# First mixer by scaled tokens and a later shift, second key chunk's weights in front of the second shift slice

## What is computed

```python
mod_l = (silu_c @ mod_w[i] + mod_b[i]).reshape(bsz, N_MOD, 1, D_MODEL)
mod_c = (silu_cc @ mod_w[i] + mod_b[i]).reshape(N_MOD, 1, D_MODEL)
h_lat = modulate(rms_norm(lat, norm_g[i, 0]), mod_l[:, 0], mod_l[:, 1])
h_ctx = modulate(rms_norm(cx, norm_g[i, 0]), mod_c[0], mod_c[1])
...
z = h.astype(jnp.float32) @ w_in
q, k, v, r, glr = jnp.split(z, [...], axis=-1)
g = jax.nn.log_sigmoid(jnp.einsum('blzr,zrk->blzk', glr, w_gate) + b_gate) / GLA_GATE_NORM
```

## Time and profile before

| | |
|---|---|
| median of 3 runs | 1206.23 us (1205.76 to 1207.28) |
| the profiled execution | 1206.26 us, of it 1204.5 us span |
| PE busy | 1158.5 us, 96% of the span |
| DVE busy | 741.7 us, 62% |
| ACT busy | 556.6 us, 46% |
| POOL busy | 113.6 us, 9% |
| mean granted clock of PE | 0.992 |
| DMA | 209.42 MB, mean 174 GB/s |

### The profile page before, as it was taken

One profiled execution on the slowest core, in us unless ns is written; L12 is line 12 of the kernel. 1 busy time (PEld: TensorE's weight loads), 2 busy tenths in 40 slices (PEclk: granted clock), 3 DMA queues, 4 the chain that ended last, 5 costly groups with the idle time before them and its releaser, 6 DMA issues.

```text
span 1204.5 us, 19086 instructions
## 1 busy us (share of the span) xinstructions
PE 1158.5 (96%) x7472; PEld 1005.1 (83%) x7476; DVE 741.7 (62%) x1048; ACT 556.6 (46%) x760; POOL 113.6 (9%) x109
## 2 busy tenths in 40 slices
PE   5899998899999989999999999999999999999997
PEld 2587775699999988648999999999999988999996
DVE  2887335697554586745465456776667776654653
ACT  3753232634333453644343346666666655433432
POOL 1000051187100070000000000000000000000000
PEclk9999999899999999999999999999999999999999
DMA  9674464977755540708554635555555434745500
GB/s 352 222 268 165 137 241 105 323 226 241 213 181 179 172 99 1 279 2 282 207 185 168 222 105 144 137 141 156 157 157 157 147 130 161 271 170 205 190 19 36
DMA packets 200241, 209.42 MB, mean 174 GB/s; under 512 B 6027, under 2 KB 167190, under 8 KB 199990
## 3 DMA queue, kind: packets, MB, share of 16 engines
q1 hardware_dynamic: 196480, 197.41, 51.3%
q0 software_dynamic: 2928, 9.02, 2.7%
q10 hardware_dynamic: 774, 2.17, 0.5%
HBM read 207.53 MB, written 2.01 MB: 174 GB/s over the span
## 4 chain that ended last, share of the span: by engine, by line
PE 90%; DVE 4%; ACT 2%; DMA 2%; issue 1%; ACTq 0%; DVEq 0%; SPq 0%
PE bank L2108 23%; PE bank L2110 23%; PE bank L2109 23%; PE bank L2378 2%; PE bank L1932 2%; PE bank L1934 2%; PE bank L1933 2%; PE bank L2505 1%; PE bank L2490 1%; PE bank L2481 1%; PE bank L2515 1%; DMA weight_pool<-in_gla_w_in_dram 1%; PE bank L1863 1%; DMA normed<-in_ctx_dram 1%; DMA weight_pool<-in_mod_w_dram 1%; PE bank L2361 1%
## 5 line engine op out<-in xcount | busy, mean ns | idle before, releaser
L2108 PE MATMUL bank<-hT_high,mlp_up_high 128*128 128x256 f32 x512 | 145.2, 284 | 0.9 <-DVE hT_low L1511 0.9
L2110 PE MATMUL bank<-hT_high,mlp_up_low 128*128 128x256 f32 x512 | 144.9, 283 | 0.0
L2109 PE MATMUL bank<-hT_low,mlp_up_high 128*128 128x256 f32 x512 | 144.9, 283 | 0.0
L2108 PE MATMUL bank<-od_w_high,hT_high 128*128 128x384 f32 x376 | 130.1, 346 | 0.0
L2110 PE MATMUL bank<-od_w_high,hT_low 128*128 128x384 f32 x376 | 126.1, 335 | 0.0
L2109 PE MATMUL bank<-od_w_low,hT_high 128*128 128x384 f32 x376 | 125.8, 334 | 0.0
L1167 DVE TENSOR_TENSOR mlp_down_low<-weight_pool,mlp_down_high 128x2048 fp32r<-128x2048 f32 x32 | 73.3, 2290 | 59.2 <-ACT mlp_down_high L690 59.2
L1167 DVE TENSOR_TENSOR od_w_low<-weight_pool,od_w_high 128x3072 fp32r<-128x3072 f32 x24 | 80.5, 3356 | 40.9 <-ACT od_w_high L690 40.9
L2108 PEld LDWEIGHTS bank<-hT_high,mlp_up_high 128*128 128x128 f32 x512 | 98.1, 192 | 2.8 <-issue 1.9
L2108 PE MATMUL bank<-hT_high,ffn_up_high 128*128 128x256 f32 x352 | 99.9, 284 | 0.0
L2108 PE MATMUL bank<-mlp_down_high,hidden_high 128*128 128x512 f32 x256 | 99.9, 390 | 0.0
(11 more groups left out here) (367 smaller groups left out, 2697.7 us busy)
## 6 DMA issues: line engine op xcount, KB each, us to landing
weight_pool<-in_mlp_w_dram SPq DMA_DIRECT2D x64, 1024.0 KB, 7.8
weight_pool<-in_od_w_in_dram SPq DMA_DIRECT2D x72, 512.0 KB, 5.2
weight_pool<-in_ffn_w_in_dram SPq DMA_DIRECT2D x44, 512.0 KB, 5.7
weight_pool<-in_mod_w_dram SPq DMA_DIRECT2D x20, 1024.0 KB, 8.1
weight_pool<-in_gla_w_in_dram SPq DMA_DIRECT2D x12, 1024.0 KB, 8.3
weight_pool<-in_ffn_w_out_dram SPq DMA_DIRECT2D x22, 512.0 KB, 7.0
weight_pool<-in_gla_w_out_dram SPq DMA_DIRECT2D x2, 2048.0 KB, 14.2
normed<-in_mod_w_dram POOLq DMA_DIRECT2D x16, 256.0 KB, 5.1
```

The source lines that it names most:

```text
L2108: mm(out_, left[0], right[0], start=start, stop=False, **flag)
L2109: mm(out_, left[0], right[1], start=False, stop=False, **flag)
L2110: return mm(out_, left[1], right[0], start=False, stop=stop, **flag)
```

## The change

Slices 2 and 3 (the scale) are fetched and computed first, then the first key chunk, slice 0, the second key chunk, slice 1. The first key chunk is no longer split: PE multiplies tokens that are only scaled (`tokens_scaled`) by the raw weights in full float32, with slices 0 and 1 and their turns in between (`scaled_keys`). The shift's share of these keys is a product of the shift columns with the same weights, turned into columns and added when DVE reads the banks. The shifted tokens (`tokens_shifted`) are made later, for the gates and all other chunks. The second key chunk is the first split one (`gla_second_chunk`), and the gate products stand in it. POOL's high part and DVE's low part of chunk 0 go. Six zero products stand ahead of the first transposes in place of ten ahead of the gates' product; ACT loads its square root table earlier; slices 4 to 7 come after chunks 3, 5, 7 and 9 in place of 1, 3, 5 and 7; and the queues of ACT and DVE are in a new order.

```diff
 SLOT = 2048
 SLOTS = 5
 GLA_CHUNKS = [("k", 0), ("k", 1), ("q", 0), ("q", 1)] + [(x, i, half) for x in "vr" for i in range(2) for half in range(2)]
-GLA_USED = [("proj_ps", 2), ("proj_ps", 4), ("proj_ps", 6), ("proj_ps", 8), ("half_used", 1), ("proj_ps", 12), ("half_used", 2),
+GLA_USED = [("glr_ps", 1), ("proj_ps", 4), ("proj_ps", 6), ("proj_ps", 8), ("half_used", 1), ("proj_ps", 12), ("half_used", 2),
             ("proj_ps", 16), ("half_used", 3), ("proj_ps", 18), ("half_used", 4), ("proj_ps", 20)]
-LATE_AFTER = {1: (4,), 3: (5,), 5: (6,), 7: (7,)}
+FIRST_SLICES = (2, 3, 0, 1)
+LATE_AFTER = {3: (4,), 5: (5,), 7: (6,), 9: (7,)}
 SUM_SLICES = (10, 11)
 POOL = 18432
...
         spread = work[:, 11520:11648]
+        scaled = view(work, 6144, KD, 512)
+        shift_rows = work[:, 5120:5376]
...
-        for i in range(4):
-            ring_slice(i)
-        for c in range(len(GLA_CHUNKS)):
+        ring_slice(2)
+        ring_slice(3)
+        ring_weights(0)
+        for half in range(2):
+            L["mod", 0, half] = plan(f"mod0_{half}", 10240 + SLOT * half, [(0, (4, 512), mod_v[:, 4 * half:4 * half + 4, 0, :])],
+                                     ("mod_rows", slice_count(0)), ring=f"w_mlp{2 + half}")
+        ring_weights(1)
+        ring_slice(1)
+        for c in range(2, len(GLA_CHUNKS)):
             ring_weights(c)
             for i in LATE_AFTER.get(c, ()):
...
-            first = L[GLA_CHUNKS[0]]
-            g.wait_ge(first.sem, first.value)
-            g.wait_ge(s["hT_dve"], 6)
-            for half in range(2):
-                at = SLOT // 2 * half
-                g.tensor_copy(gla_high[0][:, at:at + SLOT // 2], pool[:, first.at + at:first.at + at + SLOT // 2]).then_inc(s["gla_hi_first"], 1)
...
+            def tokens_scaled(k, n):
+
+                cols = slice(256 * n, 256 * n + 256)
+                src = bank[k // 2][:, 256 * (k % 2):256 * (k % 2) + 256] if n else turned[:, k, cols]
+                return act.activation(scaled[:, k, cols], src, ACT.Copy, scale=eff[:, n, k:k + 1])
...
             norm_stats(0, xn, s["ctx_loaded"], 16)
-            mod_copy(0)
+            mod_copy(2)
             norm_stats(1, res, s["x_loaded"], 16)
             tokens_out(0)
-            mod_copy(1)
+            mod_copy(3)
+            act.wait_ge(s["hT_act"], 2)
+            act.wait_ge(s["eff_ready"], 2)
+            for k in (0, 1):
+                tokens_scaled(k, 0)
+            for k in (0, 1):
+                act.wait_ge(s["xT_ps"], 4 + k // 2 + 1)
+                tokens_scaled(k, 1).then_inc(s["hT_act"], 1)
+            act.wait_ge(s["eff_ready"], 4)
+            for k in (4, 5):
+                act.wait_ge(s["xT_ps"], 4 + k // 2 + 1)
+                tokens_scaled(k, 0)
+                tokens_scaled(k, 1).then_inc(s["hT_act"], 1)
             tokens_out(1)
-            mod_copy(2)
-            mod_copy(3)
-            act.wait_ge(s["eff_ready"], 2)
-            act.wait_ge(s["hT_act"], 4)
-            act.wait_ge(s["hT_dve"], 4)
...
+            def tokens_shifted(ks):
+
+                for k in ks:
+                    for n in range(2):
+                        cols = slice(256 * n, 256 * n + 256)
+                        ins = act.activation(hT_all[:, k, cols], turned[:, k, cols], ACT.Identity, scale=eff[:, n, k:k + 1], bias=mods[:, k, 1 - n:2 - n])
+                ins.then_inc(s["hT_act"], 1)
+
...
             def gla_split_high(c):
                 e = L[GLA_CHUNKS[c]]
                 act.wait_ge(e.sem, e.value)
-                if c >= 2:
+                if c >= 3:
                     act.wait_ge(s[GLA_USED[c - 2][0]], GLA_USED[c - 2][1])
                 act.activation(gla_high[c % 2][:, :], pool[:, e.at:e.at + SLOT], ACT.Copy).then_inc(s["gla_hi"], 1)
-            for half in range(2):
-                act.wait_ge(s["hT_act"], 5 + half)
-                act.wait_ge(s["hT_dve"], 5 + half)
-                act.activation(gla_hT[0][:, 2048 * half:2048 * half + 2048], work[:, 15104 + 2048 * half:17152 + 2048 * half], ACT.Copy)\
-                   .then_inc(s["gla_hT_hi"], 1)
+            mod_copy(0)
+            act.wait_ge(s["mod_cols"], 3)
+            act.wait_ge(s["hT_act"], 8)
+            act.wait_ge(s["hT_dve"], 8)
+            tokens_shifted((0, 2))
             gla_split_high(1)
+            tokens_high(0)
+            mod_copy(1)
+            act.wait_ge(s["mod_cols"], 4)
+            tokens_shifted((4, 6))
+            tokens_high(1)
+            gla_split_high(2)
             def gate_inputs(z):
...
             gate_inputs(0)
+            gla_split_high(3)
             gate_exp(0)
             gate_inputs(1)
-            gla_split_high(2)
+            gla_split_high(4)
             gate_exp(1)
             for z in range(2):
                 act.activation(G2[:, z], G2[:, z], ACT.Ln, bias=1.0).then_inc(s["gate_ln"], 1)
...
-            gla_split_high(3)
             mod_copy(4)
-            gla_split_high(4)
+            gla_split_high(5)
             gate_exponents(0)
             gate_to_end(0)
-            gla_split_high(5)
+            gla_split_high(6)
             mod_copy(5)
             gate_exponents(1)
             gate_to_end(1)
-            gla_split_high(6)
             gla_split_high(7)
+            gla_split_high(8)
             mod_copy(6)
-            gla_split_high(8)
             gla_split_high(9)
+            gla_split_high(10)
             mod_copy(7)
-            gla_split_high(10)
             gla_split_high(11)
             for j in range(4):
...
+            norm_scale(0, xn, xn)
+            norm_scale(1, res, rG, tiles=(0,))
+            tokens_out(0)
+            mod_reduce(2)
+            norm_scale(1, res, rG, tiles=(1,))
+            scale_half(0)
+            dve.wait_ge(s["hT_dve"], 2)
+            for k in (2, 3):
+                tokens_scaled(k, 0)
+            mod_reduce(3)
+            scale_half(1)
+            for k in (2, 3):
+                tokens_scaled(k, 1).then_inc(s["hT_dve"], 1)
+            for k in (6, 7):
+                tokens_scaled(k, 0)
+                tokens_scaled(k, 1).then_inc(s["hT_dve"], 1)
+            tokens_out(1)
+            chain(dve.memset(reset, 1.0))
+            chain(dve.memset(reset[:, ::2 * SEQ], 0.0))
+            chain(dve.memset(reset[:, 0:2048].rearrange("p (h c i) -> p h c i", c=8, i=CHUNK)[:, :, 4:8, 0], 0.0))
+            mod_reduce(0)
+            dve.wait_ge(s["mod_cols"], 3)
+            dve.wait_ge(s["hT_act"], 8)
+            dve.wait_ge(s["hT_dve"], 8)
+            tokens_shifted((1, 3))
+            tokens_low(0)
+            mod_reduce(1)
+            dve.wait_ge(s["mod_cols"], 4)
+            dve.tensor_copy(silc[:, :, 2:4], mods[:, 0:KD, :]).then_inc(s["vec_cols"], 1)
+            tokens_shifted((5, 7))
             dve.wait_ge(s["glr_ps"], 1)
+            dve.tensor_copy(shift_rows, bank[2][:, 0:256]).then_inc(s["glr_ready"], 1)
+            dve.wait_ge(s["glr_ps"], 2)
             dve.tensor_copy(glr_parts, bank[0][:, :]).then_inc(s["glr_ready"], 1)
...
-                if j < 4:
+                if j < 2:
+                    for n in range(2):
+                        cols = slice(256 * n, 256 * n + 256)
+                        ins = dve.tensor_scalar(kT[:, j, cols], b[:, cols], key_shift[:, j, 1 - n:2 - n], None, ALU.add)
+                elif j < 4:
                     ins = dve.tensor_copy(kT[:, j, :], b[:, :])
...
-            gla_split_low(0)
-            gate_abs(0)
-            dve.wait_ge(s["xT_ps"], 8)
-            chain(dve.memset(reset, 1.0))
-            chain(dve.memset(reset[:, ::2 * SEQ], 0.0))
-            chain(dve.memset(reset[:, 0:2048].rearrange("p (h c i) -> p h c i", c=8, i=CHUNK)[:, :, 4:8, 0], 0.0))
             gla_split_low(1)
-            gate_abs(1)
+            dve.wait_ge(s["glr_ps"], 3)
+            shifts = bank[3][:, 0:256].rearrange("p (c g q) -> p c q g", c=2, g=4)[:, :, 2:4, :]
+            chain(dve.tensor_reduce(key_shift, shifts, AX, ALU.add))
+            tokens_low(1)
+            dve.wait_ge(s["glr_ps"], 4)
+            dve.tensor_copy(glrT, bank[1][:, :]).then_inc(s["glr_ready"], 1)
             proj(0)
             proj(1)
             gla_split_low(2)
+            gate_abs(0)
+            proj(2)
+            proj(3)
+            gla_split_low(3)
+            gate_abs(1)
+            proj(4)
+            proj(5)
+            gla_split_low(4)
             gate_logs(0)
-            proj(2)
             gate_scan(0)
             gate_ends(0)
-            proj(3)
-            gla_split_low(3)
-            gate_to_ends(0)
-            proj(4)
-            proj(5)
-            mod_reduce(4)
-            gla_split_low(4)
-            gate_logs(1)
             proj(6)
             proj(7)
+            mod_reduce(4)
+            gla_split_low(5)
+            gate_to_ends(0)
+            gate_logs(1)
             gate_scan(1)
             gate_ends(1)
-            gla_split_low(5)
+            gla_split_low(6)
             gate_to_ends(1)
```

(93 more changed lines are left out.)

118 lines of the change are left out of this document (57 added, 61 removed).

## The result

The changed kernel takes **1225.5 us** (median of 4 runs, 1224.4 to 1227.0), the kernel before 1206.1 in the same session: a ratio of 1.0158, 95% interval 1.0146 to 1.0171. Forecast were 1222.7 us, 1214.5 to 1228. The profiled execution took 1226.01 us, its span is 1224.2. That second profile (span 1221.5, called **the control** here) is what the experiments are held against.

A forecast was written before the change was run, and what follows sets the result against it. PE was taken to bound the kernel, apart from weight waits in the front. A front gain of 4.1 us, then late gates: chunk 6 12.0 later, plus 4.5, makes 16.5 on 1206.26: 1222.7 us, range 1214.5 to 1228.

The forecast's parts named there:

- First key product: In the front: PE starts the keys at 24.6 us, following DVE's scale columns at 23.0.
- A float32 product: Key chunk 0 on PE: 0.86 us per full float32 product, bounds 0.80 and 1.05; 16 products take 13.8 us.
- Waits in the keys: PE in the front: 1.0 us for the tenth transfer, 0.7 for ACT's copy of slice 1.
- End of the front: PE through both key chunks and gate products at 62.4 us, against 66.5 before: a gain of 4.1, bounds 1 and 6.
- rival of a slower front: Weights late, products near 1.05 us, PE at low clock while keys wait for tokens: 1227.7 us; chance 0.12.
- Step 1: SP's queue: slice 4's weights wait for both key tiles, so the first value chunk lands at 72.5 us.
- Step 2: ACT makes the value chunk's high part before second exp and ln(0), done 79.5; PE starts chunk 4 at 76.9, waiting 1.1.
- Step 3: Inside chunk 4: query-bank reads stand behind DVE's gate logs and scan, so PE waits 5.9 us, until 88.3.
- step 4: Before chunk 5: its low part stands behind slice 4's sum, which waits for PE's turn; PE waits 3.0 us.
- Step 5: Before chunk 6: DVE has 20.1 us of work until the value-bank read, PE 12.8; PE waits 7.3 us.
- Behind chunk 6: Up to the input products' end: 4.5 us more, from clock 1.7, one slice and turn 1.9 + 0.5, chunk 10's weights 0.4.
- The clock: PE's granted clock drops after long pauses: 1.7 us in chunk 4 and 1.7 behind chunk 6's start, bounds 0 and 3.3 each.

The follow-up runs named there:

- the control: The same changed kernel, no edit, measured and profiled again in a later session: 1224.1 us, 1.0149 times the kernel before.
- first set: The first measurement of the changed kernel, no further edit, 4 runs against the kernel before: median 1225.5 us, ratio 1.0158.
- first execution: The profiled execution of the changed kernel in its first measurement, no further edit: 1226.01 us.
- three moves: Changed kernel with DVE's query reads before gate logs and scan, slice 4's sum behind chunk 5's low part, value reads before second-half gate ends: 1208.4 us.
- the query reads alone: Changed kernel with DVE's reads of the query banks moved ahead of the first half's gate logs, scan and ends: 1216.5 us.
- best order: Kernel with the three moves and slice 1's weights ahead of key chunk 1's, slice 4's sum moved on behind the reads of tiles 8 to 11: 1202.5 us.
- the sum further back: Changed kernel with slice 4's sum on DVE moved behind the low parts of both chunks 5 and 6: 1218.0 us.

## Why the prediction was right

It named the three waits, their places, their releasers and their order, and the runs that take each away confirm it. The first set's 1225.5 us lie 2.8 above the forecast, the control's 1224.1 1.4 above. By its steps, against the control:

- **First key product** 24.6 forecast, 25.4 measured: 0.8 late, as DVE's scale columns were ready at 23.9 and not at 23.0.
- **A float32 product** 0.86 forecast. The sixteen take, without what stands between them, 5.32 + 0.96 + 2.67 + 0.96 + 4.38 = 14.3 us, 0.89 each: 0.5 us more. The Trainium skill (FP8 and Floating Point Precision, TensorE Precision Notes), whose four passes gave 0.92 and 14.7 by my estimate, is as near as the row I took; the measurement lies between them.
- **Waits in the keys** 1.0 and 0.7 forecast, 1.75 measured, all of it on the transfer and none on ACT's copy. That the sums agree is luck: the tenth transfer let PE go on at 39.5, not 37.5, PE itself came about a microsecond later than forecast, and ACT's copy was in time.
- **End of the front** 62.4 forecast, 63.6 measured: the front wins 2.9 us, not 4.1. This is the mis-sized term, the two entries above (0.8 + 0.5). The first execution showed only 0.7: 1.7 more went to the clock at 40 to 44 us, for which the sum had no term (only the rival of a slower front spoke of a low clock in the keys), and 0.5 to a later transfer. The early loss at 18 to 22 us is gone, as forecast: the clock is 1.00 there.
- **Step 1** value chunk at 72.5 forecast, 73.2 measured.
- **Step 2** ln(0) at 79.5 forecast, 80.1 measured. Chunk 4 starts at 77.5 (76.9 forecast); the wait in front of it is 0.3 and not 1.1, since PE itself came later. The table load takes 1.28 us, from 76.92, and ln starts right behind, at 78.22. The 2.66 us with a drain that the Trainium skill gives (ScalarE: Activation LUTs, What ACT_TABLE_LOAD costs) do not show here, and were rightly left out of the sum.
- **Step 3** wait of 5.9 forecast, 5.6 measured; **step 4** 3.0 and 2.7; chunk 5 at 98.9 and 99.5.
- **Step 5** chunk 6 at 119.0 forecast, 119.6 measured. The wait is 5.4 and not 7.3, as the clock, low again behind step 4's wait, spread PE's 12.8 us over 14.6. The text had that loss as hidden, which it is: it changes the wait's size, not its end.
- **Behind chunk 6** 4.5 forecast; (171.58 - 119.60) - (154.56 - 107.01) = 4.4 measured. Here too errors cancel: the clock took 1.8 (chunk 6's tiles 12.8 us against 11.0), the slice and the turn, what is left, 2.6 and not 2.4, and chunk 10 did not wait (0.4 forecast; 0.7 in the first execution).
- **The clock** 1.7 behind a long wait; 1.85 measured by itself.

So chunk 6 is 12.6 us late against 12.0, and the control ends 17.0 us later than before at the input products, 16.5 forecast. The 1.4 us between the medians of the two sets of this kernel may be the clock in the front, which only the profiled execution of each shows.

One side remark was wrong: that swapping slice 1 and key chunk 1 changes the total by under 2 us. It is 3.8 us here, and from the kernel with three moves to that with the swap too, 1208.4 - 1203.2 = 5.2 (at the end of the input products 2.7 and 4.2). I had counted slice 1's own wait (1.7) but not that the order of transfers also decides which places the next ones wait for.

## What to carry to other kernels

When a producer of data moves later, go through each in-order queue behind it and ask, of every step, when its input comes and who waits for what stands behind it: reads that free a bank belong in front of work that is not yet due, and a step that waits for another engine belongs behind all that this engine will need. A busy share of 55% says nothing against an engine being the one that is waited for. And a wait should be moved past everything it could block, not by one place: by one place the input products ended 1.7 us earlier, by six 9.4.

## What was not expected of the hardware

- PE's clock cost nearly as much behind a wait of 2.7 us as behind one of 5.4. Chunk 5 up to slice 5 takes 11.1 us after a wait of 1.52 (three moves at once) and after none (slice 4's sum behind one low part), and 12.7 after one of 2.69 (the query reads alone). Chunk 6's four tiles take 11.0 us without a wait (best order) and after one of 1.63 (the sum further back), and 12.8 to 13.2 after one of 5.4.
- The cost of one and the same wait differs between executions. The last two tiles of chunk 4 take 5.62 us at full clock. Behind the wait of 5.5 to 5.6 us they took 7.4 in the first profile, 7.5 in the control, 7.7 and 7.9 with slice 4's sum moved by one place and by six, and 8.4 with the value reads moved, though up to there the order is the same in all five: 1.8 to 2.8 us.
- The clock can differ where the timeline so far is the same: 0.58 or 1.00 from 40 to 42 us, behind waits of 1.76 and 1.79. That is 1.7 us in 1225, as much as many an edit.
- Zero products of 5.35 us in all, put into a wait, held the clock at 1.00, and gave back 1.85 us on the spot.
